# Order of key and value products inside the second layer's attention bursts on TensorE

## The chip, the cores and the metric

One core of a Trainium2 chip runs the whole program. The metric is the device time of one execution in microseconds (us), as the median of several. TensorE (PE in the rows; PEld is its weight load) multiplies, VectorE (DVE) and ScalarE (ACT) do the elementwise work and empty PSUM banks, GpSimd (POOL) issues the attention's small transfers, and SyncE (SP) issues the stream of weights from HBM.

## The reference, cut to what matters

Two transformer blocks run one after the other on 512 tokens of width 2048. The change lies in the second block, which has 16 heads of a dilated attention and 16 heads of a neighbourhood attention, each head 64 wide:

```python
def second_block(x, w_in, w_out, t5_bias, na_rpb, ln_gain, ln_bias):
    h = jnp.einsum('bsd,de->bse', x, w_in[layer])
    qa, ka, va, ga, qb, kb, vb, gb = jnp.split(h, splits, axis=-1)
    ya = _dilated_attention(heads(qa), heads(ka), heads(va), t5_bias)       # softmax(q k + bias) v
    yb = _neighbourhood_attention(heads(qb), heads(kb), heads(vb), na_rpb)  # the same in windows of an 8 x 64 grid
    y = concatenate([merge(ya) * silu(ga), merge(yb) * silu(gb)])
    out = jnp.einsum('bse,ed->bsd', y, w_out[layer])
    x = _layer_norm(DEEPNORM_ALPHA * x + out, ln_gain[layer], ln_bias[layer])
```

For each head a product of queries and keys gives logits, a softmax over them gives probabilities, and a product of probabilities and values gives the head's output.

## The kernel before

Every engine has its own instruction stream, written out by hand, and the streams meet in semaphores. TensorE's order is therefore exactly the order in the code.

In the second layer, `w_in` is taken in 16 steps, each for a pair of heads: steps 0 to 7 compute the queries, keys, values and gates of the dilated pairs (kind "A2"), steps 8 to 15 those of the neighbourhood pairs ("M2" on TensorE, "N2" elsewhere). A step is four chunks of weights, each 48 matmuls of 128x512 (every product is three matmuls: high part times high part, low times high, high times low; lines 458 to 460). A chunk's weights are split into the high part by ScalarE (line 442) and the low part by VectorE (line 447).

The attention of the pair computed in step n-1 runs inside step n, in **bursts** between those chunks (`beat`, line 1192). For A2 there are two bursts in a step, in front of chunks 0 and 2, each with half of the pair's query blocks; for M2 there is one, in front of chunk 0, with all four. A burst holds:

- key products (`qk2`, line 1161): matmuls of 64 rows, two heads side by side, 12 in an A2 burst (128x512) and 24 in an M2 burst (128x256). They give the logits, in PSUM banks 2 to 5.
- value products (`pv2`, line 1182): 32 matmuls of 64 columns, two heads side by side, from turned probabilities `prob_t` (two slots, waited for apart) and value tokens. They write bank 6.

Logits go to VectorE (`soft2_a`, lines 2478 and 2482: bias and maximum), ScalarE (exponential, line 1712) and VectorE again (`soft2_b`: division; `flip2`: a turn in blocks), then through POOL to HBM and back (`flip_d`, then `prob_t`, line 3023), and come back as `prob_t` for a later burst's value products: one burst later for A2, a whole step later for M2. So a burst's values never use the same burst's keys. VectorE empties the chunk's banks (lines 2595 to 2616) ahead of the softmax in its own order, and multiplies the value products by the gate (`gated2`, lines 2524 and 2531) behind it.

After the loop one more burst stands alone (lines 1276 to 1286): the keys of the last pair (step 16) and the values of pair 15, and then the first products with `w_out` (`early_products`, line 1264). There VectorE's order is: softmax of the first two blocks, the low part of one weight chunk, the low part of four tiles of attention output (line 2394), softmax of the other two blocks, divisions and turns of all four, `gated2` of pair 15, low parts of more attention output (lines 2539 and 2394; ScalarE makes their high parts between), and then the low part of the third chunk of `w_out` (line 447).

Of the kernel before, what the change touches and what calls it, by code (L numbers as in the profile page):

```python
# [137 lines left out]
def build_kernel(nc, wst, xt_in, mem_in, par_in, con_in, pos_in, tab1_in, tab2_in, rpb_in, lng_in, lnb_in, out):  # L138
# [25 lines left out]
    with ctx:  # L164
# [263 lines left out]
        def w_part(c, i):  # L428

            a11, a12, _, a22 = w_quarters(c)  # L430
            return (a11, a12, a22)[i] if i < 3 else s_sum[i - 3][:]
# [59 lines left out]
        def tb_of(k):  # L491
            return TB - 1 - k
# [18 lines left out]
        def unit_of(step, cc):  # L511

            return 4 * step + (cc - 4)

        def evac_act(step, half):

            return 2 * step + (52 + half)

        def evac_dve(step, half):

            return 2 * step + (28 + half)
# [12 lines left out]
        def at2(kind, cc):  # L534

            return (cc % 2, 0) if kind == "A2" else (cc // 2, 256 * (cc % 2))

        def qk_lo(att, par):

            return (qk_lo_a if att == "A2" else qk_lo_n)[par]  # L540

        def logit_bank(kind, step, cc, e):

            if kind == "A2":
                return bank[2 * (cc % 2) + 2 + e]
            return bank[2 * (cc // 2) + 2 + e]
# [5 lines left out]
        def flips(kind, step, cc):  # L552

            return 32 * step + (16 * (cc // 2) - 16) if kind == "A2" else 16 * step + 128
# [6 lines left out]
        def v2_loads(kind, step):  # L561

            return 16 * step if kind == "A2" else 96 * step - 640
# [111 lines left out]
        def _(pe):  # L675
# [470 lines left out]
            def qk2(kind, step, cc, par):  # L1146

                u, off = unit_of(step, cc), at2(kind, cc)[1]
                (q_h, k_h), (q_l, k_l) = qkvg[par][0:2], qk_lo(kind, par)
                c, w = (tb_of(cc), 512) if kind == "A2" else (cc, 256)  # L1150

                def keys(t, half):

                    if kind == "A2":
                        return t[half, :]
                    return t[half, :].rearrange("p (r c) -> p r c", c=64)[:, :, BLK_START[cc]:BLK_START[cc] + 32]

                for n, (q, k) in enumerate(((q_h, k_h), (q_l, k_h), (q_h, k_l))):
                    for e in range(2):
                        half = slice(64 * e, 64 * e + 64)  # L1160
                        ins = pe.matmul(logit_bank(kind, step, cc, e)[:, off:off + w], q[half, c * P:(c + 1) * P], keys(k, half),  # L1161
                                        start=(n == 0), stop=(n == 2))
                        if n == 2:
                            ins.then_inc(s2_ready, 1)

            def pv2(kind, step, cc, par):

                slot = at2(kind, cc)[0]
                if kind == "A2":
                    c, n, v = tb_of(cc), 4, v_tok_a[par][:]  # L1170
                    turned = prob2_t[slot][:].rearrange("p i (e b q) -> p e b i q", e=2, b=4)
                else:
                    c, n, v = cc, 2, v_tok_n[par][:, cc]
                    turned = prob2_t[slot][:].rearrange("p i (e c b q) -> p c e b i q", e=2, c=2, b=2)[:, cc % 2]
                pe.wait_ge(iq_loaded[slot], PROB2_T0 + flips(kind, step, cc))
                if cc == 0:
                    pe.wait_ge(v2_loaded, v2_loads(kind, step))
                    if not (isinstance(step, int) and step == 1):
                        pe.wait_ge(o2_ready, step - 1)
                for b in range(n):  # L1180
                    for e in range(2):
                        last = pe.matmul(bank[O_BANK][64 * e:64 * e + 64, c * P:(c + 1) * P],  # L1182
                                         v[:, b, 64 * e:64 * e + 64], turned[:, e, b],
                                         start=(b == 0), stop=(b == n - 1), skip_group_check=True)
                if cc % 2 == 1:
                    last.then_inc(pv2_ready, 1)
# [5 lines left out]
            def beat(kind, before, step, pair, par):  # L1192

                if pair == 0:
                    pe.wait_ge(ev_dve, evac_dve(step - 1, 0))
                    pe.wait_ge(x1l_s, step + 8)
                if pair or before:
                    pe.wait_ge(l2_ready, 2 * unit_of(step, 2 * pair))
                for cc in range(4) if kind == "M2" else (2 * pair, 2 * pair + 1):
                    qk2(kind, step, cc, par)  # L1200
                if kind == "A2" and pair:
                    for cc in range(2):
                        pv2("A2", step, cc, par)
                elif before == "A2" and pair == 0:
                    for cc in range(2, 4):
                        pv2("A2", step - 1, cc, 1 - par)
                elif before == "M2":
                    for cc in range(4):
                        pv2("M2", step - 1, cc, 1 - par)

            def pair_step(step, par, kind, before, gemm=True):

                for cc in range(4):
                    if kind and (cc == 0 or (cc == 2 and kind == "A2")):
                        beat(kind, before, step, cc // 2, par)
                    g = 2 * step + (G_IN2 + cc // 2)
                    if cc % 2 == 0 and before and (cc == 0 or kind == "A2"):
                        pe.wait_ge(ev_act, evac_act(step, cc // 2 - 1))
                        pe.wait_ge(ev_dve, evac_dve(step, cc // 2 - 1))
                    elif cc == 2 and kind == "A2":  # L1220
                        pe.wait_ge(ev_act, evac_act(step, 0))
                        pe.wait_ge(ev_dve, evac_dve(step, 0))
                    chunk_ready(pe, 2 * g + cc % 2)
                    if cc == 2 and kind == "M2":
                        for n in range(2):
                            if n:
                                pe.wait_ge(ev_act, evac_act(step, 0))
                            for k in range(4):
                                mm3(pe, bank[in2_banks(kind, cc)[n]][:], wt(w_hi[0], k, n * P, P), wt(w_lo[0], k, n * P, P),
                                    act_b[0][:, k, :], act_b[1][:, k, :], start=(k == 0), stop=False)  # L1230
                        rows_t(pe, 0, range(4, 6), act_b, in2_banks(kind, cc))
                    else:
                        rows_t(pe, cc % 2, range(6), act_b, in2_banks(kind, cc))
                    if cc == 1 and not kind:
                        pe.wait_ge(x1h_s, 10)
                        pe.wait_ge(x1l_s, 8)
                    rows_t(pe, cc % 2, range(6, 8), act_b, in2_banks(kind, cc)).then_inc(chunk_used, 1)
# [39 lines left out]
            pe.wait_ge(ev_dve, evac_dve(15, 0))  # L1277
            pe.wait_ge(l2_ready, 2 * unit_of(16, 0))
            for cc in range(4):
                qk2("M2", 16, cc, 1)  # L1280
            for cc in range(4):
                pv2("M2", 15, cc, 0)
            pe.wait_ge(ev_act, evac_act(15, 1))
            pe.wait_ge(ev_dve, evac_dve(15, 1))
            early_products(0, range(4))
# [518 lines left out]
        def _(dve):  # L1804
# [31 lines left out]
            def rows_copied(jobs):  # L1836

                for n in jobs:
                    _, _, a, b, dst = BIAS_JOBS[n]
                    dve.wait_ge(pb_s, n - n % 2 + 2)  # L1840
                    dve.tensor_copy(dst, bank[n % 4][0:dst.shape[0], 0:b - a]).then_inc(pe_s, 1)
# [1313 lines left out]
```

## Time and profile before

| | us |
|---|---|
| median of 3 runs | 2454.0 (2453.28 to 2454.55) |
| the profiled execution, its own time | 2453.05 |
| its span, first to last instruction | 2451.5 |
| PE busy | 2439.3 |
| PEld busy | 2086.8 |
| DVE busy | 1520.4 |
| ACT busy | 840.1 |
| POOL busy | 683.8 |

The chain of work that ended last is 97% PE. The granted clock of TensorE is 0.999 of its full 2.4 GHz over the span. Busy time of PE counts overlapping matmuls once, and their ends are modelled; what a burst costs is therefore read from the starts of its matmuls and not from durations.

### The profile page before, as it was taken

How to read it: one execution, taken by the hardware profiler on the slowest of the kernel's cores; microseconds unless marked ns; L12 is line 12 of the kernel's file. 1: busy time of each engine (PE TensorE's matmuls, PEld its weight loads, DVE VectorE, ACT ScalarE, POOL GpSimd, SP SyncE). 2: the span in 40 equal slices, each digit the busy share in tenths (PEclk: the TensorE clock that was granted, in tenths of full speed). 3: DMA queues.
4: the chain of work that ended last, by engine and by line, in shares of the span. 5: the costliest groups of instructions: out<-in, count | busy, mean ns of one | idle time of the engine just before them, and what ended most of it. 6: DMA issues, size and time to landing. Idle time of an engine off the chain costs nothing.

```text
span 2451.5 us, 36158 instructions
## 1 busy us (share of the span) xinstructions
PE 2439.3 (100%) x13712; PEld 2086.8 (85%) x13712; DVE 1520.4 (62%) x2529; ACT 840.1 (34%) x1281; POOL 683.8 (28%) x867
## 2 busy tenths in 40 slices
PE   9999999999999999999999999999999999999998
PEld 7798999999978888888888888888888888888886
DVE  5676878898779876556554433555565546555535
ACT  7322445545453433323212222232232323223220
POOL 0313556666412232321001320212122423333100
PEclk9999999999999999999999999999999999999999
DMA  7759333433457666777444444666656555546622
GB/s 289 223 176 299 113 127 126 135 130 130 147 165 239 237 234 238 247 252 264 162 164 155 147 144 118 216 199 200 198 187 209 187 163 158 181 158 211 246 88 103
DMA packets 102149, 451.48 MB, mean 184 GB/s; under 512 B 18006, under 2 KB 18070, under 8 KB 73926
## 3 DMA queue, kind: packets, MB, share of 16 engines
q1 hardware_dynamic: 38712, 241.58, 28.5%
q0 software_dynamic: 63312, 208.20, 26.6%
q8 instruction: 82, 1.34, 0.2%
q14 instruction: 43, 0.35, 0.0%
HBM read 350.94 MB, written 100.26 MB: 184 GB/s over the span
## 4 chain that ended last, share of the span: by engine, by line
PE 97%; DVE 2%; DMA 1%; SPq 0%; ACT 0%; issue 0%; DVEq 0%
PE bank L458 22%; PE bank L459 22%; PE bank L460 22%; PE bank L875 16%; PE bank L1264 5%; PE bank L1182 2%; PE bank L1320 2%; PE bank L1161 2%; PE bank L1044 1%; PE bank L1019 1%; DMA w_raw<-wst 1%; PE bank L956 1%; PE bank L1039 0%; PE bank L1009 0%; DVE w_lo L447 0%; DVE k_nat L1810 0%
## 5 line engine op out<-in xcount | busy, mean ns | idle before, releaser
L447 DVE TENSOR_TENSOR w_lo<-w_raw,w_hi 128x2048 fp32r<-128x2048 f32 x164 | 375.8, 2291 | 332.3 <-ACT w_hi L442 330.0
L458 PE MATMUL bank<-act_b,w_hi 128*128 128x512 f32 x1280 | 500.8, 391 | 0.0
L459 PE MATMUL bank<-act_b,w_lo 128*128 128x512 f32 x1280 | 498.3, 389 | 0.0
L460 PE MATMUL bank<-act_b,w_hi 128*128 128x512 f32 x1280 | 498.0, 389 | 0.0
L442 ACT ACTIVATE w_hi<-w_raw 128x2048 fp32r<-128x2048 f32 x163 | 311.8, 1913 | 454.2 <-PE bank L460 365.1
L458 PE MATMUL bank<-act_a,w_hi 128*128 128x512 f32 (+2 forms) x1032 | 398.8, 386 | 0.3 <-DVE w_lo L447 0.3
L459 PE MATMUL bank<-act_a,w_lo 128*128 128x512 f32 (+2 forms) x1032 | 394.8, 383 | 0.0
L460 PE MATMUL bank<-act_a,w_hi 128*128 128x512 f32 (+2 forms) x1032 | 394.7, 382 | 0.0
L458 PEld LDWEIGHTS bank<-act_b,w_hi 128*128 128x128 f32 x1280 | 240.2, 188 | 53.6 <-issue 4.1
L460 PEld LDWEIGHTS bank<-act_b,w_hi 128*128 128x128 f32 x1280 | 240.3, 188 | 50.3
L459 PEld LDWEIGHTS bank<-act_b,w_lo 128*128 128x128 f32 x1280 | 240.3, 188 | 49.1
L875 PE MATMUL bank<-t_xh,pt_w 128*128 128x256 f32 x1280 | 232.1, 283 | 0.0
L458 PEld LDWEIGHTS bank<-act_a,w_hi 128*128 128x128 f32 (+1 forms) x1032 | 193.4, 187 | 38.2 <-issue 2.1
L460 PEld LDWEIGHTS bank<-act_a,w_hi 128*128 128x128 f32 (+1 forms) x1032 | 193.4, 187 | 36.2
L459 PEld LDWEIGHTS bank<-act_a,w_lo 128*128 128x128 f32 (+1 forms) x1032 | 193.5, 188 | 34.0
L875 PEld LDWEIGHTS bank<-t_xh,pt_w 128*128 128x128 f32 x1280 | 199.7, 192 | 0.0
L875 PE MATMUL bank<-act_a,pt_w 128*128 128x256 f32 x1440 | 181.5, 283 | 0.0
L875 PE MATMUL bank<-t_xl,pt_w 128*128 128x256 f32 x640 | 181.1, 283 | 0.0
L875 PEld LDWEIGHTS bank<-act_a,pt_w 128*128 128x128 f32 x1440 | 176.2, 192 | 3.0 <-DVE pt_w L2110 2.1
L2110 DVE TENSOR_TENSOR pt_w<-s_sum,pt_w 128x512 fp32r<-128x512 f32 x160 | 155.2, 983 | 36.9 <-ACT pt_w L1333 36.3
L2789 POOL TENSOR_TENSOR s_sum<-w_raw 128x512 f32<-128x512 f32 x80 | 119.8, 1508 | 109.2 <-DMA w_raw<-wst 63.9
L1333 ACT ACTIVATE pt_w<-s_sum 128x512 fp32r<-128x512 f32 x160 | 100.6, 630 | 94.1 <-PE bank L875 79.8
(376 smaller groups left out, 3352.9 us busy)
## 6 DMA issues: line engine op xcount, KB each, us to landing
w_raw<-wst SPq DMA_DIRECT2D x210, 1024.0 KB, 5.0
prob_t<-flip_d POOLq DMA_DIRECT2D x64, 512.0 KB, 4.7
flip_d<-flip POOLq DMA_DIRECT2D x56, 512.0 KB, 4.2
mix_d<-stage POOLq DMA_DIRECT2D x24, 512.0 KB, 3.3
mixg<-mix_d POOLq DMA_DIRECT2D x8, 1536.0 KB, 6.8
prob_tk<-flip_d POOLq DMA_DIRECT2D x32, 256.0 KB, 5.8
flip_d<-flip_a POOLq DMA_DIRECT2D x16, 512.0 KB, 2.9
b<-rows_2d POOLq DMA_DIRECT2D x16, 448.0 KB, 10.3
```

The costliest lines, as they stand in the source:

```text
L442: act.activation(w_hi[s][:], w_raw[s][:], ACT.Copy).then_inc(hi_ready, 1)
L447: dve.tensor_tensor(w_lo[s][:], w_raw[s][:], w_hi[s][:].bitcast(F32), ALU.subtract).then_inc(lo_ready, 1)
L458: pe.matmul(out_ap, l_hi, r_hi, start=start, stop=False)
L459: pe.matmul(out_ap, l_lo, r_hi, start=False, stop=False)
L460: return pe.matmul(out_ap, l_hi, r_lo, start=False, stop=stop)
L875: last = pe.matmul(quarter(g, i), pt_w[i][l][:, j, :], x_part(c, i, r, j), start=(i % 2 == 0 and c == 0 and j == 0 and m == 0), stop=(c == ...
L1161: ins = pe.matmul(logit_bank(kind, step, cc, e)[:, off:off + w], q[half, c * P:(c + 1) * P], keys(k, half), start=(n == 0), stop=(n == 2))
L1182: last = pe.matmul(bank[O_BANK][64 * e:64 * e + 64, c * P:(c + 1) * P], v[:, b, 64 * e:64 * e + 64], turned[:, e, b], start=(b == 0), stop ...
L1264: last = pe.matmul(bank[4 * s + b][:], act_b[l][:, k, b * P:(b + 1) * P], wt(r[c % 2], kt, 0, 2 * GC, 2 * GC), start=(k == 0 and n == 0), ...
L1333: return act.activation(dst, src, ACT.Copy, **kw)
L2110: dve.tensor_tensor(pt_w[i][1][:], w_part(c, i), pt_w[i][0][:].bitcast(F32), ALU.subtract)\
L2789: pool.tensor_tensor(dst[:], l, r, op).then_inc(ws_s, 1)
```

## The change

In every burst the value products move in front of the key products; the waits that each of them had move with it. Nothing is added or removed.

```diff
                 if pair or before:
                     pe.wait_ge(l2_ready, 2 * unit_of(step, 2 * pair))
-                for cc in range(4) if kind == "M2" else (2 * pair, 2 * pair + 1):
-                    qk2(kind, step, cc, par)
                 if kind == "A2" and pair:
...
                     for cc in range(4):
                         pv2("M2", step - 1, cc, 1 - par)
+                for cc in range(4) if kind == "M2" else (2 * pair, 2 * pair + 1):
+                    qk2(kind, step, cc, par)
...
             for cc in range(4):
+                pv2("M2", 15, cc, 0)
+            for cc in range(4):
                 qk2("M2", 16, cc, 1)
-            for cc in range(4):
-                pv2("M2", 15, cc, 0)
```

TensorE's order at the first burst of an A2 step in the loop, as a difference (L1198 is the wait for read logits, L1175 the wait for the first slot of `prob_t`; `x8` counts equal instructions in a row):

```order
 L1196 REGISTER_ALU
 L1198 ISA
+L1175 ISA
+L1182 MATMUL bank<-prob_t_160,v_tok_a_153 64x128 x8
+L1182 MATMUL bank<-prob_t_161,v_tok_a_153 64x128 x8
 L1161 MATMUL bank<-qkvg_130,qkvg_129 128x512 x2
 L1161 MATMUL bank<-qkvg_130,qk_lo_a_135 128x512 x2
```

The wait for the probabilities and the value products now stand behind the wait for read logits and in front of the first key product; behind the key products the same rows are gone, and the chunk's own waits follow them directly.

TensorE's order at the burst of step 16, before (the end of the burst):

```order
L1161 MATMUL bank<-qkvg_130,qkvg_129 128x256 x2
L1161 MATMUL bank<-qkvg_130,qk_lo_n_139 128x256 x2
L1161 MATMUL bank<-qk_lo_n_140,qkvg_129 128x256 x2
L1182 MATMUL bank<-prob_t_160,v_tok_n_155 64x128 x8
L1182 MATMUL bank<-prob_t_161,v_tok_n_155 64x128 x8
L1264 MATMUL bank<-w_hi_51,act_b_57 128x512
```

And TensorE's order there now (the start of the burst; the first row ends the loop):

```order
L1246 COMPARE_AND_BRANCH
L1182 MATMUL bank<-prob_t_160,v_tok_n_155 64x128 x8
L1182 MATMUL bank<-prob_t_161,v_tok_n_155 64x128 x8
L1161 MATMUL bank<-qkvg_130,qkvg_129 128x256 x2
L1161 MATMUL bank<-qkvg_130,qk_lo_n_139 128x256 x2
L1161 MATMUL bank<-qk_lo_n_140,qkvg_129 128x256 x2
```

The 32 value products went from the end of this burst, next to the output products (L1264), to its start. On VectorE, ScalarE, GpSimd and SyncE no row of the order differs.

## Rows read from the trace of the kernel before

**Rows 1.** The page, part 1: busy us (share of the span) xinstructions.

```profile
PE 2439.3 (100%) x13712; PEld 2086.8 (85%) x13712; DVE 1520.4 (62%) x2529; ACT 840.1 (34%) x1281; POOL 683.8 (28%) x867
```

**Rows 2.** Waits of PE: line, waited for; us in total, times, longest.

```profile
PE bank L743 <- POOL warm L2705: 1.6, 1, 1.6
...
PE bank L458 <- DVE w_lo L447: 0.3, 1, 0.3
```

**Rows 3.** Timeline of PE, an A2 burst: start us, us, engine, line, operation [idle].

```profile
1699.34 0.39 PE L459 MATMUL bank<-act_b,w_lo 128*128 128x512 f32 x1
1699.57 0.39 PE L460 MATMUL bank<-act_b,w_hi 128*128 128x512 f32 x1
1699.88 0.50 PE L1161 MATMUL bank<-qkvg,qkvg 64*128 64x512 f32 x2
1700.22 0.40 PE L1161 MATMUL bank<-qkvg,qk_lo_a 64*128 64x512 f32 x2
...
1701.15 0.39 PE L1161 MATMUL bank<-qk_lo_a,qkvg 64*128 64x512 f32 x2
1701.47 1.97 PE L1182 MATMUL bank<-prob_t,v_tok_a 128*64 128x128 f32 x32
1703.37 0.50 PE L458 MATMUL bank<-act_b,w_hi 128*128 128x512 f32 x1
```

**Rows 4.** Timeline of PE, the first burst of all, which holds keys alone.

```profile
1524.64 0.40 PE L1161 MATMUL bank<-qk_lo_a,qkvg 64*128 64x512 f32 x2
1524.96 0.50 PE L458 MATMUL bank<-act_b,w_hi 128*128 128x512 f32 x1
```

**Rows 5.** Timeline of PE, the last value products of all, behind output products.

```profile
2296.47 0.39 PE L1264 MATMUL bank<-w_lo,act_b 128*128 128x512 f32 x1
2296.79 1.97 PE L1182 MATMUL bank<-prob_t,v_tok_n 128*64 128x128 f32 x32
```

**Rows 6.** DMA issues in 1588 to 1598 us: xcount, KB each, median us to landing.

```profile
w_raw<-wst SPq DMA_DIRECT2D x1, 1024.0 KB, 10.7
...
prob_t<-flip_d POOLq DMA_DIRECT2D x1, 512.0 KB, 8.2
```

**Rows 7.** Timelines of POOL and PE: that load's issue, and the burst that needs it.

```profile
1588.27 0.77 POOL L3023 DMA_DIRECT2D prob_t<-flip_d  x1 [0.78 <-DMA flip_d<-flip_a]
...
1597.93 0.50 PE L1161 MATMUL bank<-qkvg,qkvg 64*128 64x512 f32 x2
...
1599.51 1.97 PE L1182 MATMUL bank<-prob_t,v_tok_a 128*64 128x128 f32 x32
```

**Rows 8.** Timeline of POOL: the later load of probabilities in the last M2 step.

```profile
2237.59 0.78 POOL L3023 DMA_DIRECT2D prob_t<-flip_d  x1 [6.71 <-DMA flip_d<-flip_n]
```

**Rows 9.** Timeline of PE: the burst of step 16 and two later output products.

```profile
2260.36 0.39 PE L1161 MATMUL bank<-qkvg,qkvg 64*128 64x256 f32 x2
...
2261.07 0.29 PE L1161 MATMUL bank<-qk_lo_n,qkvg 64*128 64x256 f32 x2
...
2262.02 1.97 PE L1182 MATMUL bank<-prob_t,v_tok_n 128*64 128x128 f32 x32
2263.92 0.73 PE L1264 MATMUL bank<-w_hi,act_b 128*128 128x512 f32 x2
...
2269.50 0.61 PE L1264 MATMUL bank<-w_hi,act_b 128*128 128x512 f32 x2
...
2285.82 0.61 PE L1264 MATMUL bank<-w_hi,act_b 128*128 128x512 f32 x2
```

**Rows 10.** Timeline of DVE behind that burst.

```profile
2261.98 0.42 DVE L2482 CUSTOM_DVE_ANT_0 prob<-bank,nb 128x256 f32<-128x256 f32 x1
...
2265.99 2.28 DVE L2394 TENSOR_TENSOR act_b<-o_raw,act_b 128x2048 fp32r<-128x2048 f32 x1
...
2277.93 0.69 DVE L2539 TENSOR_TENSOR act_b<-o_st,act_b 128x512 fp32r<-128x512 f32 x1 [0.70 <-ACT act_b L1333]
...
2282.89 2.28 DVE L447 TENSOR_TENSOR w_lo<-w_raw,w_hi 128x2048 fp32r<-128x2048 f32 x1
```

## The prediction

> **What bounds the kernel now.** I read the page's busy times first, then the waits of PE, then the starts of PE's matmuls in the bursts, and last the engines that feed a burst. PE is busy for 2439.3 of the 2451.5 us of the span [rows 1]. It waits four times in the whole program, 1.6 us at the start and three times under 1 us; of these only the 0.3 us could be in a loop at all [rows 2], and none is at a burst. So PE is the bound in the stage of the change, and no burst waits for its probabilities, for its logit banks or for a chunk of weights. Two things follow. A reordering on PE can't gain time by removing a wait, because there is none. It can change the time in two ways only: through what PE itself spends when it goes from one kind of product to another, or by making something late that is now just early enough.
>
> **What the burst costs on PE.** I use starts, since ends are modelled. In the A2 burst shown [rows 3] chunk products follow each other at 0.23 us (1699.34 to 1699.57). From the last of them to the first key product it is 0.31, so the change of kind costs about 0.09. The key products take 1.59 us to the first value product (1699.88 to 1701.47), and in it their pitch is 0.23 (four pitches from 1700.22 to 1701.15) but the last one, to the values, is 0.32: again 0.09. The values take 1.90 us to the next chunk product. Now the new order: chunk to values, values to keys, keys to chunk.
> - Chunk to values is shown once: 0.32 from the output product to the last value run [rows 5], against 0.31 for chunk to keys. Difference +0.01 at most.
> - Keys to chunk is shown in the first burst, which has no values: 0.32 from the last key product [rows 4], the same as keys to values. Difference 0.
> - Values to keys is shown nowhere. The nearest row is values to chunk, inside the 1.90 of [rows 3]; with it the burst costs what it did.
>
> So a burst costs 0 to +0.01 us more, and there are 23 bursts with both kinds (15 of A2 alone, one of M2 keys with A2 values, 7 of M2 alone): at most +0.2, and I take +0.1 us. The unknown step is bounded by its neighbours: if going from values to keys cost nothing extra, 23 x 0.09 = 2.1 us would be saved; if it cost twice as much, 2.1 us would be lost. I take the same 0.09, because all four changes of kind that rows show cost that, whichever the kinds. The Trainium skill ("TensorEngine Tiling (Array Packing)", Key Properties) says that changing the tiling mode drains TensorE, and counts 64-row and 64-column tiles as different modes. By that rule the unseen change is as dear as the others and the lower bound falls away; the visible changes agree with it at 0.09 us each. The waits move too, but their cost on PE's queue does not show now: the last value run stands behind waits of its own and starts after 0.32 all the same [rows 5].
>
> **What comes due earlier: the probabilities.** Values start where keys started, so they need their `prob_t` 1.59 us earlier in A2 [rows 3] and 1.66 in M2 (2260.36 to 2262.02) [rows 9]. **What comes later: the logits.** Keys start when the values are through, 1.90 us later, so softmax, turns and transfers of the A2 pair can be up to 1.90 later (less where VectorE was still emptying banks). Together a load may lose 3.49 us of its slack in A2. M2 has plenty: the later of the two loads for the burst at 2260.36 [rows 9] is issued at 2237.59 [rows 8], 22 us ahead. In A2 the worst load is that of the second slot for the burst at 1597.93: issued at 1588.27 [rows 7], 8.2 us in flight [rows 6], so landed at about 1596.5. With its logits 1.90 later it lands at 1598.4. The second slot is wanted by the second half of the values only: half of a run of 1.97 less one product is about 0.85 us (an estimate from [rows 3]) behind 1597.93, so at 1598.8. It is early by 0.4 us in the worst case. I take 0 for the A2 bursts and 0 to 1 us for the range. The first slot is loaded first and has more. Of the queues: POOL issues these loads in the same order as before, its stores of the flips just move with VectorE; SyncE's weight loads wait for the low parts (line 447), which stand behind the first softmax and move at most 1.90 us, while the chunk that they fill is needed two chunks later, over 20 us (48 matmuls at 0.23 us are 11 us a chunk). Bank emptying stays ahead of the softmax on VectorE and is not moved, so the chunk behind a burst does not wait.
>
> **What has no such cover: the step 16 burst.** There the softmax of the last pair heads a chain on VectorE that PE needs within the next 22 us. First its shift. Logits of the first two blocks are read together, and are complete with the sixth pair of key products, at 2261.07 + 0.29 = 2261.36 [rows 9]; the softmax started at 2261.98 [rows 10], because banks were emptied until then. With keys 1.90 later (2262.02 to 2263.92 is what the values take) the logits come at 2263.26, so the softmax starts 1.28 later. VectorE works without a gap from there to the low parts at line 2394, which ended at 2265.99 + 2.28 = 2268.27 [rows 10]; they will end at 2269.55. PE wants them for its second chunk of early products at 2269.50 [rows 9]: 0.05 us late. The same 1.28 goes on through divisions and turns to `gated2`, from there through ScalarE's high parts (VectorE waits for ScalarE there, and ScalarE for `gated2`: 0.70 idle at 2277.93) to the low part of the third `w_out` chunk. That one ended at 2282.89 + 2.28 = 2285.17 [rows 10], and PE started the third chunk at 2285.82 [rows 9]: 0.65 us early. It will end at 2286.45, so PE waits 0.63, the 0.05 included. Nothing gives it back, as PE is the bound behind it. The next link has room: the last values follow at 2296.79 [rows 5].
>
> **The sum.** Against the profiled execution, 2453.05 us (span 2451.5 and 1.55 around it): +0.1 at the changes of kind, 0 at the probabilities, +0.6 at step 16: 2453.75. The median of the runs, 2454.0, is 0.95 above the profiled one, so the forecast is **2454.7 us**, no change that can be measured. The limits of the unknown terms are -2.1 to +2.1, 0 to +1, and 0 to +1.3 (the whole shift of step 16 if its cover were used up).
>
> **The rivals.**
> - *The change from values to keys is free.* For it: nothing shows that change, and each product kind already uses the array in halves. Against it: keys to values is also from one half to another, and costs 0.09 [rows 3]. It would give 2454.7 - 2.1 = 2452.6, still no change.
> - *Step 16 does not slip*, because something in VectorE's chain, which I read as gapless, gives the 1.28 us back before 2282.89. For it: three short idle times of VectorE for ScalarE lie there. Against it: ScalarE's own work in them follows from VectorE's. It would give 2454.1.
> - *The probabilities come late (slower).* VectorE's shift moves the load of the second slot into the weight load that runs beside it: that one took 10.7 us in the same stretch [rows 6]. Were the probabilities' load to take as long, it would land at 1588.27 + 1.90 + 10.7 = 1600.9, 2.1 us too late. It decides from a flight of 8.6 us. Eight bursts (the second of each A2 step) have this place, so 17 us: about 2471. Against it: the one of 8.2 is the slowest, and the 3.49 us is an upper bound.
> - *The change does not do what it says.* The instruction order shows both blocks exchanged on PE at every burst and no other engine touched, so I give this nothing.
>
> **How the numbers follow.** Forecast 0.74 (2454.7), free change of kind 0.08 (2452.6), no slip at step 16 0.10 (2454.1), late probabilities 0.05 (2471), and 0.03 for a gain that I see no place for. The first three are within 0.2% (4.9 us, about what a measurement of this kernel can tell from no change): same 0.92, slower 0.05, faster 0.03. The range goes from 2452.6 less 0.6 for the spread of the runs, 2452.0, to 2454.7 + 2.1 + 0.3 for a few short waits, 2457.1; the late probabilities stay outside.
>
> **What would show it.** Starts of PE in an A2 burst of the changed kernel: values at 0.31 behind the chunk, keys 1.90 later, the chunk 1.59 behind those; if keys follow values at the bare pitch, the second term falls. A wait of PE at line 1264 for VectorE's `w_lo` (line 447) of about 0.6 us would confirm step 16; its absence would make the second rival right. A wait of PE at line 1182 for a DMA of `prob_t` would be the slower rival, and many of them would make the prediction wrong; so would chunks behind the burst that wait for VectorE or ScalarE at lines 2595 to 2616.

## The result and the profile after

| | before | changed |
|---|---|---|
| median of 17 runs each, us | 2453.72 (2452.46 to 2456.33) | 2459.08 (2455.06 to 2463.14) |
| ratio, 95% interval | | 1.002 (1.0013 to 1.0026) |
| the profiled execution, its own time, us | 2453.05 | 2463.05 |
| its span, us | 2451.5 | 2461.5 |

The changed kernel is slower by 5.4 us in the median, and its runs are spread over 8 us where those of before lie within 4. The profiled execution of the changed kernel is one of its slowest, 10.0 us over the one of before. I go through that one first, since its rows show every kind of loss, and leave the median to the experiments.

Waits of PE in the changed kernel (line, waited for; us in total, times, longest), to be read against [rows 2]:

```profile
PE bank L1182 <- DMA prob_t<-flip_d: 4.8, 2, 3.2
PE bank L743 <- POOL warm L2705: 1.6, 1, 1.6
PE bank L458 <- DVE w_lo L447: 1.4, 4, 0.5
...
PE bank L1264 <- issue: 0.4, 1, 0.4
...
PE bank L1264 <- DVE act_b L2394: 0.2, 1, 0.2
```

Value products now wait for their probabilities, chunks wait for low parts four times instead of once (two of the four, 0.9 us, lie ahead of the second block's first burst), and the products with `w_out` wait twice. First, though, a burst in which nothing is late, timeline of PE (start us, us, engine, line, operation), against [rows 3]:

```profile
1705.68 0.39 PE L460 MATMUL bank<-act_b,w_hi 128*128 128x512 f32 x1
1706.00 1.97 PE L1182 MATMUL bank<-prob_t,v_tok_a 128*64 128x128 f32 x32
1707.89 0.50 PE L1161 MATMUL bank<-qkvg,qkvg 64*128 64x512 f32 x2
...
1709.16 0.40 PE L1161 MATMUL bank<-qk_lo_a,qkvg 64*128 64x512 f32 x2
1709.49 0.50 PE L458 MATMUL bank<-act_b,w_hi 128*128 128x512 f32 x1
```

From the last chunk product to the next: 0.32 + 1.89 + 1.60 = 3.81 us. Before it was 0.31 + 1.59 + 1.90 = 3.80. The order itself costs 0.01 us a burst.

A burst whose second slot of probabilities is late, same view:

```profile
1650.10 1.09 PE L1182 MATMUL bank<-prob_t,v_tok_a 128*64 128x128 f32 x16
1654.36 1.09 PE L1182 MATMUL bank<-prob_t,v_tok_a 128*64 128x128 f32 x16 [3.17 <-DMA prob_t<-flip_d]
1655.39 0.59 PE L1161 MATMUL bank<-qkvg,qkvg 64*128 64x512 f32 x2
...
1657.48 0.63 PE L1161 MATMUL bank<-qk_lo_a,qkvg 64*128 64x512 f32 x2
1658.05 0.79 PE L458 MATMUL bank<-act_b,w_hi 128*128 128x512 f32 x1
```

The run of values takes 5.29 us to the first key product instead of 1.90: 3.4 us lost. The keys behind it take 2.66 instead of 1.59. The reason stands in the view of stretches (us; busy time and count of PE, PEld, DVE, ACT, POOL; granted clock; DMA share; GB/s):

```profile
1653.00:1656.00 3.00, 1.64 (x20) 1.37 (x22) 0.00 (x0) 0.09 (x1) 0.00 (x0) 0.94 0.80 176
1656.00:1659.00 3.00, 3.00 (x12) 1.94 (x11) 1.95 (x7) 0.59 (x1) 0.00 (x0) 0.50 0.15 50
```

After the wait TensorE was granted half its clock, 1.2 GHz, for about 3 us, which cost 1.5 us more: 1.1 in the keys, the rest in the chunk products behind them. The load that was late and what ran beside it, as rows of GpSimd, of SyncE, and of the load's time to landing:

```profile
1642.67 0.77 POOL L3023 DMA_DIRECT2D prob_t<-flip_d  x1 [0.43 <-issue]
...
1643.74 0.33 SPq L635 DMA_DIRECT2D w_raw<-wst  x1
...
prob_t<-flip_d POOLq DMA_DIRECT2D x1, 512.0 KB, 11.6
```

The load took 11.6 us; the slowest in the profile of before took 8.2 [rows 6]. SyncE's weight load of 1 MB was issued 1.07 us behind it. In the profile of before the weight load followed the load of [rows 7] at 3.30 us (SyncE's row there: 1591.57). For the load that is late here, that of the burst in step 3, the distance was 2.14 us before, the shortest of all the second-slot loads for the second bursts of steps 2 to 8:

```profile
1640.41 0.77 POOL L3023 DMA_DIRECT2D prob_t<-flip_d  x1 [1.88 <-DMA flip_d<-flip_a]
...
1642.55 0.33 SPq L635 DMA_DIRECT2D w_raw<-wst  x1
```

The second late burst, at 1909.86, has a load of 10.4 us with a weight load 1.39 behind, and costs 1.9.

In the M2 steps the loss comes by another road. Timelines of GpSimd, VectorE and PE in one step of the changed kernel:

```profile
2107.91 5.59 POOL L2982 TENSOR_TENSOR nb<-nl,con 128x256 f32<-128x256 f32 x8
...
2107.55 8.09 DVE L447 TENSOR_TENSOR w_lo<-w_raw,w_hi 128x2048 fp32r<-128x2048 f32 x1 [0.90 <-ACT w_hi L442]
...
2115.79 0.47 PE L458 MATMUL bank<-act_b,w_hi 128*128 128x512 f32 x1 [0.32 <-DVE w_lo L447]
```

A low part of a chunk, 2.28 us elsewhere [rows 10], lasts 8.09 while GpSimd adds the window bias of the next pair, and PE waits for it (0.71 us from the matmul ahead instead of 0.23: 0.48 lost). This happens in two of the six M2 steps, 0.9 us together.

At step 16, VectorE and PE, against [rows 9] and [rows 10]:

```profile
2272.25 0.42 DVE L2482 CUSTOM_DVE_ANT_0 prob<-bank,nb 128x256 f32<-128x256 f32 x1 [0.47 <-PE bank L1161]
...
2276.27 2.29 DVE L2394 TENSOR_TENSOR act_b<-o_raw,act_b 128x2048 fp32r<-128x2048 f32 x1
...
2293.32 2.28 DVE L447 TENSOR_TENSOR w_lo<-w_raw,w_hi 128x2048 fp32r<-128x2048 f32 x1
...
2278.70 0.70 PE L1264 MATMUL bank<-w_hi,act_b 128*128 128x512 f32 x2 [0.24 <-DVE act_b L2394]
...
2295.70 0.70 PE L1264 MATMUL bank<-w_hi,act_b 128*128 128x512 f32 x2 [0.43 <-issue]
```

The softmax now waits for its logits, and PE stops at both places that the prediction named. The last row names no engine, but the low part above it ended at 2295.60, 0.10 us ahead of the product. By starts, 0.62 and 0.82 us from the product ahead instead of 0.23: 0.4 and 0.6 lost.

Some of the loss lies ahead of the first burst that the change touches. The last key product of the first burst of all, timeline of PE:

```profile
1525.84 0.40 PE L1161 MATMUL bank<-qk_lo_a,qkvg 64*128 64x512 f32 x2
```

The sum of the profiled execution is the following: 1.2 us lost ahead of the first burst (its last key product starts at 1525.84, against 1524.64 in [rows 4]; up to there the change has moved no instruction of PE, and the same row stands at 1524.83 with values first in A2 alone, at 1529.11 with step 16 alone), 3.4 + 1.5 + 1.9 in two late bursts, 0.9 in the M2 steps, 1.0 at step 16: 9.9 of the 10.0.

### The profile page after: what moved, and what is told of

Same layout as the page of the kernel before. It is cut to its first block, busy times and chain, and to the rows that moved or that the text cites. A ratio compares the mean times of both kernels' runs of the same rounds, so it can differ in the third digit from the quotient of the medians.

```text
span 2461.5 us, 36162 instructions
## 1 busy us (share of the span) xinstructions
PE 2442.4 (99%) x13712; PEld 2087.8 (85%) x13712; DVE 1515.8 (62%) x2529; ACT 840.8 (34%) x1281; POOL 686.7 (28%) x867
## 4 chain that ended last, share of the span: by engine, by line
PE 91%; DVE 4%; DMA 3%; SPq 1%; issue 1%; ACT 0%; POOL 0%; DVEq 0%; POOLq 0%; ACTq 0%
PE bank L458 20%; PE bank L459 20%; PE bank L460 20%; PE bank L875 16%; PE bank L1264 5%; PE bank L1182 2%; PE bank L1320 2%; PE bank L1161 2%; DVE w_lo L447 1%; DMA prob_t<-flip_d 1%; PE bank L1044 1%; DMA raw_m<-wst 1%; DMA rows_b<-rows_1b 1%; PE bank L1019 1%; DMA x_raw_q<-x_d 1%
## 5 line engine op out<-in xcount | busy, mean ns | idle before, releaser
L447 DVE TENSOR_TENSOR w_lo<-w_raw,w_hi 128x2048 fp32r<-128x2048 f32 x164 | 391.8, 2389 | 305.2 <-ACT w_hi L442 302.6
```

Source lines behind the costliest of these rows:

```text
L447: dve.tensor_tensor(w_lo[s][:], w_raw[s][:], w_hi[s][:].bitcast(F32), ALU.subtract).then_inc(lo_ready, 1)
```

## The experiments

My theory after the result: the new order costs PE nothing by itself, and the whole loss comes from three things that were just in time, the probabilities of the second slot in A2, the low parts beside the window bias in M2, and VectorE's chain at step 16. The rival: a cost of the order in every burst, which the starts do not show.

**The change in parts.** The first three kernels have values first in one kind of burst only. The edit of the first (the others have `before == "M2"`, or the exchange at step 16 alone):

```diff
-                for cc in range(4) if kind == "M2" else (2 * pair, 2 * pair + 1):
-                    qk2(kind, step, cc, par)
+                if not (before == "A2" or pair):
+                    for cc in range(4) if kind == "M2" else (2 * pair, 2 * pair + 1):
+                        qk2(kind, step, cc, par)
...
+                if (before == "A2" or pair):
+                    for cc in range(4) if kind == "M2" else (2 * pair, 2 * pair + 1):
+                        qk2(kind, step, cc, par)
```

> Values first in the 16 bursts with A2 values alone; the six bursts with M2 values in the loop and the burst of step 16 as before. Late-probability theory: nearly all of the loss is here, +3 to +4.5 us against before in the median (2457 to 2458), single runs spread over 5 us or more, and in the profile one or more waits of PE at line 1182 for the load of prob_t into the second slot, 1 to 4 us each; the order values to keys to chunk itself costs within 0.01 us of before. Rival (a hidden cost of the new order, the same in each of 23 bursts, 0.23 us each): +3.7 us as well, but with the same narrow spread as before, and no wait.

> Values first in the six bursts of the loop that have M2 values alone. Theory that the window bias of GpSimd starts later and holds up the low part of a chunk on VectorE: 0 to +2 us, from waits of PE at line 458 for w_lo of about 0.5 us in some of the steps. Rival (the same hidden cost in each burst, 0.23 us): +1.4 us with no wait. If the 2 us shift of the softmax reaches no one: 0.

> Values first in the burst of step 16 alone. Theory of the VectorE chain: +1.0 to +1.2 us, as waits of PE at line 1264 (0.4 for act_b of line 2394, 0.6 for w_lo of line 447) in every run, and no other wait. Rival (the same hidden cost in each burst): +0.2 us, no wait. As predicted before the result: +0.6 us.

> The whole change once more, beside its parts on the same chip. Late-probability theory: +4 to +6.5 us in the median, the sum of the three parts within 1.5 us, with a spread of 5 us or more from run to run; the profile has another set of late bursts than the first one, since which load is late is a matter of the transfers around it. Rival (hidden cost in each burst): +5.4 us, narrow.

Measured on one chip, against a median of before of 2453.50. The last column is the time in the profile from the last key product of the first burst (the first row of [rows 4]) to the end of the span, less the 926.9 us that it takes in the kernel before. It leaves out what varies ahead of that product, which starts between 1524.6 and 1529.1 in the profiles of this document.

| values first in | median, us | all runs | ratio, 95% interval | behind the first burst, us |
|---|---|---|---|---|
| A2 bursts (16) | 2457.06 | 2453.67 to 2467.96 | 1.0020 (1.0008 to 1.0031) | +7.6 |
| M2 bursts of the loop (6) | 2455.19 | 2454.16 to 2456.57 | 1.0007 (0.9998 to 1.0016) | +1.1 |
| step 16 alone | 2455.26 | 2454.09 to 2458.49 | 1.0006 (0.9997 to 1.0015) | +0.9 |
| all (the change again) | 2464.04 | 2457.83 to 2466.69 | 1.0034 (1.0023 to 1.0045) | +11.4 |

The A2 bursts carry the wide spread, as the theory wanted. The parts add to +7.0 us; the whole is +10.5 here and was +5.4 in the first comparison, so two of my expectations were missed: that the whole would lose 4 to 6.5 us, and that the parts would add up to it within 1.5. The size of the loss is itself a matter of which loads are late, and it differs from one set of runs to another. The medians of the M2 bursts and of step 16 alone are not clear of noise, as their intervals reach below 1; what these two cost is read from the profiles. For the A2 bursts and the whole change the profiled execution is among the slower runs, so the last column stands above the median there. The rival, 0.23 us in each burst, would make step 16 alone cost 0.2, and its profile shows 0.9, with two waits; what it would make of the A2 bursts is tested below.

The waits of PE in the A2 kernel:

```profile
PE bank L1182 <- DMA prob_t<-flip_d: 5.0, 4, 2.3
```

in the profile of the whole change again,

```profile
PE bank L1182 <- DMA prob_t<-flip_d: 6.2, 3, 2.2
```

and in the M2 kernel, one of its low parts, with GpSimd beside it:

```profile
2242.51 8.03 DVE L447 TENSOR_TENSOR w_lo<-w_raw,w_hi 128x2048 fp32r<-128x2048 f32 x1 [0.90 <-ACT w_hi L442]
...
2242.82 5.57 POOL L2986 TENSOR_TENSOR nb<-nl,con 128x256 f32<-128x256 f32 x8
...
2250.68 0.47 PE L458 MATMUL bank<-act_b,w_hi 128*128 128x512 f32 x1 [0.25 <-DVE w_lo L447]
```

The M2 kernel has one more wait, of 0.4 us by starts, at the third chunk of `w_out`. The kernel with step 16 alone stops at the same two products as the whole change (0.60 and 0.66 us from the one ahead), and nowhere else in the second layer.

**What slows the load of probabilities.** The flight of a load is the time from its issue to its landing, and its lead is the time from its issue to that of the weight load behind it. In the profile of before, the second-slot loads of the first half of steps 2 to 8 have leads of 2.1 to 3.5 us and flights of 5.0 to 8.2. In three profiles with A2 values first the leads are 1.1 to 2.0. All seven flights over 10 us (10.4 to 11.6) are among these, with leads of 1.06 to 1.53; where the lead is 1.7 or more, most flights are 5 to 6 us. The weight load does not move: it is issued 6.36 us ahead of the burst before (1642.55 and 1648.91 in step 3) and after (1643.74 and 1650.10), because the low part that it follows waits for ScalarE's high part, and that one for PE to be done with a chunk. The load of probabilities moves towards it with the later logits, by 1.1 to 2.1 us in the profile of the changed kernel. But GpSimd's bias loads are there too, 0.8 to 2 us behind, in the same queue. Two kernels tell them apart. In the first, SyncE waits:

```diff
...
+            def weight_group(g, behind_turns=False):
                 for s in range(2):
                     sp.wait_ge(lo_ready, 2 * g + s - 1)
+                    if behind_turns and s == 0:
+                        sp.wait_ge(iq_loaded[1], 16 * g - 1072)
                     sp.dma_start(w_raw[s][:], wst[2 * g + s]).then_inc(w_loaded[s], 16)
...
+            with sp.Fori(72, 88) as g:
+                weight_group(g, behind_turns=True)
...
```

> The run of A2 bursts with values first (e1_a2_only), and SyncE's weight load that follows the second load of probabilities waits until that one has landed (steps 1 to 8, both halves). Theory that the weight load, which now starts 1.2 to 1.7 us behind the load of probabilities instead of 2.1 to 3.5, slows it: no load of prob_t takes over 8.5 us, no wait of PE at line 1182, the time within 0.5 us of before and its spread as narrow (2452.5 to 2456). Rival (the bias loads of GpSimd's own queue, 0.8 and 1.4 us behind, slow it): flights of 9 to 11 us remain in some bursts, 2 to 4 us slower than before.

Measured: 2453.51 us (2452.68 to 2454.43) against 2453.90, ratio 0.9999 (0.9990 to 1.0008). PE has no wait at line 1182, and no flight exceeds 8.3 us; the weight load is 4.4 us or more behind. Behind the first burst the profile is level with before (926.8 us), so 16 bursts in the new order cost nothing by themselves, and the rival of a cost in each burst falls. All waits of PE:

```profile
PE bank L752 <- POOL warm L2718: 1.6, 1, 1.6
PE bank L458 <- DVE w_lo L447: 1.3, 2, 0.9
PE bank L458 <- DVE w_lo L1875: 0.7, 1, 0.7
PE bank L458 <- DVE w_lo L1840: 0.3, 1, 0.3
```

All of them lie ahead of the first burst. VectorE's low part, which runs beside the load, is not what slows it: in this kernel, as in the changed one, 15 of the 16 second-slot loads are issued while that low part runs, and here none is late. In the second kernel GpSimd waits with the bias loads instead:

```diff
+                    if kind == "A2":
+                        pool.wait_ge(iq_loaded[1], PROB2_T0 + flips(kind, step, 1))
+                        pool.nop(nofuse=True)
                     bias_load(following, step + 1, 1 - par)
```

> The same A2 bursts, the weight loads as before, and instead GpSimd's two bias loads (and the store of the attention output behind them) wait until the second load of probabilities has landed. If the weight load alone slows it: as e1_a2_only, +2 to +4 us, flights of 9 to 11 us where the weight load is less than 1.6 us behind. If the bias loads slow it: no flight over 8.5 us, no wait at line 1182, within 0.5 us of before. If both have to be there: no waits either, and then e4 has none as well.

Measured: 2453.96 us against 2453.90, ratio 1.0000 (0.9991 to 1.0009), and ten of its runs within 2452.4 to 2455.4. But the eleventh, its profiled one, took 2459.96 and shows what is left: five waits at line 1182,

```profile
PE bank L1182 <- DMA prob_t<-flip_d: 4.4, 5, 1.8
```

and for the first of them the load, the weight load 0.53 us behind it, and the time to landing, with no bias load near:

```profile
1591.10 0.77 POOL L3027 DMA_DIRECT2D prob_t<-flip_d  x1 [0.39 <-issue]
...
1591.63 0.33 SPq L635 DMA_DIRECT2D w_raw<-wst  x1
...
prob_t<-flip_d POOLq DMA_DIRECT2D x1, 512.0 KB, 9.7
```

So my alternatives were too sharp. A weight load close behind can make a load late without any bias load; taking the weight load away ends it, and taking the bias loads away brings the median back. How often a load is still late then is open: the one run of eleven that shows it is the profiled one. Of the A2 kernel, whose bias loads do not wait, 9 of 12 runs are over the 2455.4 that the other ten stay within.

Nor does the weight load decide alone. In the profiles here, twelve second-slot loads with a weight load 0.5 to 1.3 us behind and no bias load near landed within 4.3 to 6.8 us, and six with one 0.5 to 1.6 us behind took 7.9 to 9.7. In the twelve the first slot's load had been issued 1.9 us or more ahead, in the six 0.8 to 1.6. So it seems to take three transfers close together; no experiment here tests that.

**The window bias.** GpSimd waits until the low part is made:

```diff
                 if following == "N2":
+                    if kind == "N2":
+                        pool.wait_ge(lo_ready, 2 * (2 * step + G_IN2 + 1) + 2)
+                        pool.nop(nofuse=True)
                     window_bias(step + 1, 1 - par)
```

> The run of M2 bursts with values first (e2_m2_only), and GpSimd's eight additions of the window bias wait until VectorE has made the low part of the third chunk of the step. Theory that they hold this low part up: the low part takes 2.3 us instead of up to 8, no wait of PE at line 458, within 0.5 us of before (e2_m2_only had +1.7). Rival (the loss of e2_m2_only lies elsewhere): +1 to +2 us.

Measured: 2453.60 us against 2453.90, ratio 1.0001 (0.9992 to 1.0010). The low part has its own length again, GpSimd follows it, and PE does not stop at a chunk of the M2 steps, nor at the third chunk of `w_out`. Behind the first burst the profile is level with before (926.8 us).

```profile
2242.93 2.29 DVE L447 TENSOR_TENSOR w_lo<-w_raw,w_hi 128x2048 fp32r<-128x2048 f32 x1 [0.91 <-ACT w_hi L442]
...
2245.50 5.59 POOL L2986 TENSOR_TENSOR nb<-nl,con 128x256 f32<-128x256 f32 x8 [2.77 <-DVE w_lo L447]
```

**The chain of step 16.** VectorE does other work while it would wait for the logits:

```diff
+            part_lo(PARTS_2, 1, len(PARTS_1))
             for cc in range(2):
                 soft2_a("M2", 16, cc, 1)
             split_lo(dve, 2 * G_OUT2 + 1, 1)
-            part_lo(PARTS_2, 1, len(PARTS_1))
```

> Values first in the burst of step 16 alone (e3_tail_only), and VectorE makes the low part of four tiles (line 2394) ahead of the softmax of the first two blocks instead of behind it and the weights' low part, so that it works while it would wait for the logits. Chain theory: the waits of PE at line 1264 (0.4 and 0.4 to 0.6 us) go, and the time is within 0.5 us of before (e3_tail_only had +1.8). Rival (the loss of e3_tail_only is not this chain): +1 to +2 us.

Measured: 2454.15 us against 2453.90, ratio 1.0001 (0.9992 to 1.0010), and no wait at line 1264. VectorE (the first row is the one that was moved):

```profile
2262.19 2.27 DVE L2394 TENSOR_TENSOR act_b<-o_raw,act_b 128x2048 fp32r<-128x2048 f32 x1
2264.38 0.41 DVE L2482 CUSTOM_DVE_ANT_0 prob<-bank,nb 128x256 f32<-128x256 f32 x1
...
2283.04 2.28 DVE L447 TENSOR_TENSOR w_lo<-w_raw,w_hi 128x2048 fp32r<-128x2048 f32 x1
```

The idle time ahead of the softmax is gone, and the low part starts 20.9 us behind the moved row's start, just as it started 20.9 us behind the softmax in the kernel before (2261.98 to 2282.89 in [rows 10]). Behind the first burst the profile is level with before (926.8 us).

**All mends, with the change and without.**

> The whole change with the three mends together: the weight load waits for the second load of probabilities (as e4), the window bias waits for the low part of the third chunk (as e6), VectorE makes four tiles' low part ahead of the softmax of step 16 (as e7). If late probabilities, the window bias and the chain of step 16 are the whole loss: within 0.5 us of before and as narrow, no wait of PE in the second layer. If something of the new order remains: the rest of +5 to +10 us that these three don't explain.

> The kernel before with the same three mends, keys first. If the mends only give back what the change lost: as before, within 0.5 us, and level with f1_after_mended. If they gain by themselves (a better flow of transfers), this is faster than before, and f1 has to be measured against this one and not against before.

Measured, against 2453.76 on the same chip: the change with the mends 2453.35 us (2452.42 to 2455.21), ratio 0.9999 (0.9990 to 1.0008), keys first with the mends 2454.57 (2452.76 to 2456.39), ratio 1.0003 (0.9994 to 1.0012). Neither differs from before beyond the interval. They are 1.2 us apart, with overlapping runs, where I expected them level; behind the first burst their profiles take 926.5 and 926.8 us. All waits of PE in the changed and mended kernel:

```profile
PE bank L458 <- DVE w_lo L1836: 2.2, 1, 2.2
PE bank L752 <- POOL warm L2714: 1.6, 1, 1.6
PE bank L458 <- DVE w_lo L447: 0.3, 1, 0.3
```

The first two are at the start of the program, the third is that of [rows 2]. The three causes are the whole loss as far as these runs can tell (2.2 us either way by the median, 0.3 by the profile behind the first burst), and the order hides no gain beyond that. No version here beats the kernel before by more than that.

**A burst split in three.** The values of the first slot, the keys, the values of the second slot, in A2 bursts alone and with nothing mended:

```diff
...
+                if vals:
+                    pv2(*vals[0])
                 for cc in range(4) if kind == "M2" else (2 * pair, 2 * pair + 1):
                     qk2(kind, step, cc, par)
-                if kind == "A2" and pair:
...
+                if vals:
+                    pv2(*vals[1])
```

> No mend and no change but the order inside the 16 bursts with A2 values: the values of the first slot, the keys, the values of the second slot. Keys are then some 1 us later than before instead of 1.9, and the second slot is wanted no earlier than before. If the loss of e1_a2_only is the second slot alone, no wait at line 1182. The price is a fourth change of kind in each burst: about 0.14 us by the starts in the trace of before (0.09 for the change, 0.05 for the first value products), so +2.2 us for 16 bursts with a narrow spread. If a change of kind costs nothing beyond what the trace shows as starts: 0; if the first slot was late too, waits at the first value product.

Measured: 2455.51 us (2454.53 to 2457.58) against 2453.76, ratio 1.0008 (0.9999 to 1.0017), no wait at line 1182. Timeline of PE in one burst:

```profile
1702.00 1.09 PE L1182 MATMUL bank<-prob_t,v_tok_a 128*64 128x128 f32 x16
1703.03 0.50 PE L1161 MATMUL bank<-qkvg,qkvg 64*128 64x512 f32 x2
...
1704.29 0.39 PE L1161 MATMUL bank<-qk_lo_a,qkvg 64*128 64x512 f32 x2
1704.61 1.09 PE L1182 MATMUL bank<-prob_t,v_tok_a 128*64 128x128 f32 x16
```

Both things that were expected are there. The second slot, wanted no earlier than in the kernel before, is not late in this profile, and neither is the first, which is wanted as early as in the changed kernel. And the fourth change of kind has its price: values 1.03, keys 1.58, values 1.02 to the next product, 3.63 us in place of 3.49 (1.59 + 1.90) [rows 3], so 0.14 in each of 16 bursts, 2.2 us. The medians differ by 1.75, which is not clear of noise by itself, and the profile behind the first burst is 1.9 longer than before.

## Why the prediction was wrong

- **PE is the bound and no wait can be won**: right. No kernel in the new order is faster than before clear of noise, and with all three causes mended it is level.
- **The cost of the order on PE, +0.1 us**: right. Values to keys, which no row of before showed, starts the keys 1.89 us behind the first value product (1.90 was taken) and the burst is 3.81 us long in place of 3.80. The rival of a free change of kind is refuted by the split burst, in which one more change cost 0.14. The Trainium skill ("TensorEngine Tiling (Array Packing)", Key Properties) says that a change of tiling mode drains TensorE. The traces agree: about 0.09 us at each change of kind that they show by single starts, 0.31 or 0.32 against 0.23 in an A2 burst.
- **The probabilities, "I take 0 for the A2 bursts and 0 to 1 us for the range"**: this is the step that failed, and most of the median's loss lies in it (+3.6 us for A2 alone, up to +14 in a run; 6.8 in the profile of the changed kernel, where the sum had 0). The arithmetic of who is wanted when was right, with 0.4 us of slack in the worst burst. But I moved the load by the shift of its logits and kept its flight of 8.2 us, and I let the weight loads "move at most 1.90 us" as well. The weight load moves by nothing, so the load of probabilities comes closer to it, from 2.1 to 3.5 us ahead of it to 1.1 to 2.0, and with that its flight grows, up to 11.6. I also looked for the worst load by its flight (step 2) and not by its distance to the next transfer: the load of step 3, which had the shortest of steps 2 to 8 (2.14 us), is late in all three profiles with A2 values first. The rival "the probabilities come late" named just this collision, a flight that decides from 8.6 us and a wait of 2.1 us; flights of 10.4 to 11.6 with waits of 1.7 to 3.2 were measured. Where it was wrong is the chance, 0.05, and the price, which set all eight bursts late in every run. In these three profiles two, three and four loads make PE wait, apart from step 3 in another place each time, and the result is a wide spread between my forecast and that rival. A case between "never" and "always" was missing.
- **M2 has plenty**: right for the probabilities (they land 13 us and more ahead), wrong for what else stands in GpSimd's queue. I followed the loads there and not the window bias behind them, which now starts late enough to fall on the next low part. That is 0.9 us in the profile of the whole change; with M2 alone it is 1.1 behind the first burst, and nothing once the additions wait.
- **Step 16, +0.63**: the mechanism was right at both places, 2269.50 and 2285.82 in [rows 9], and the experiment that fills VectorE's idle time removes it. The size was off: about 1.0 us in waits. The burst starts at 2269.21 in this execution, 8.85 us later than in [rows 9], so the rows of VectorE compare less 8.85: the softmax at 2263.40 against 2261.98 [rows 10], 1.42 later and not 1.28, and the row at line 447 at 2284.47 against 2282.89, 1.58 later. The first two products behind each of the two stops also take some 0.1 us longer by themselves (0.70 in place of 0.61).
- **Chunks behind a burst don't wait**: right; the emptying of the banks was not moved.
- **The range**, 2452.0 to 2457.1, missed 2459.08 since it left the slower rival outside whole, instead of holding the part of it in which some bursts are late. It did not hold its own limits either: those of the three unknown terms, +2.1, +1 and +1.3, add up to 2458.4.

## What to carry to other kernels

A reordering on an engine that never waits has no wait to win back, and it spends slack in two places at once: what is moved forward is wanted earlier, and what is moved back makes its successors later. Compare the sum with the slack of each transfer, and ask what other transfer it now comes close to, because a flight time read from a trace may hold only for the neighbours that it had there. When the runs of a changed kernel spread wider than before, look for a transfer that is sometimes late, and give the transfer that has time a wait.

## What I had not expected

- A wait of 3.17 us on PE was followed by about 3 us at a granted clock of 0.50, half of 2.4 GHz, which cost 1.5 us more; in the A2 kernel one of 2.16 us was followed by the same. So were waits of 2.20 and 1.94 us in the repeat of the whole change, and one of 1.81 in the kernel whose bias loads wait, but not others of 2.31, 2.01, 1.67 and 1.66. A late load can cost 1.5 us on top of the wait that the trace names, or nothing.
- VectorE's subtraction of a weight chunk, 2.29 us, took 8.09 and 8.03 us when GpSimd's additions of 5.6 us began 0.3 to 0.4 us behind its start: it ended 2.1 us after GpSimd had ended, as if it had only begun then. In the kernel before, the same additions held up another, shorter operation (line 2600: 4.9 to 5.3 us in place of 0.7), and nobody waited for it. The Trainium skill ("SBUF — State Buffer", SBUF: two separate sides) says that a VectorE operation with two inputs in SBUF and a GpSimd operation that reads SBUF lock each other out of a shared pair of ports, and that the one that starts first holds it for its whole length. The lockout agrees with the 8.09; the order does not by the recorded starts, where VectorE's was first, by 0.36 us.
